# A first stage with four adaLN weight pieces loaded at once, one piece per three token tiles, and two key units among the tiles

## The reference

```
mod = silu(cond) @ ada_w + ada_b            # cond: two vectors (latent, context); ada_w: 1024 x 3072, one per layer
shift, scale, gate = split(mod, 3)
h = rmsnorm(x, norm_w) * (1 + scale) + shift
p = h @ w_in                                # the projection: per key/value head k, v, then queries and gates
```

## Time and profile before

| | |
|---|---|
| median of 3 runs | 2668.88 us |
| lowest, highest | 2666.84, 2669.97 us |
| profiled execution | 2663.45 us, of which the span of the profile 2661.6 us |
| TensorE products busy | 2588.9 us, 97% |
| TensorE weight loads busy | 2268.2 us, 85% |
| VectorE | 1187.3 us, 45% |
| ScalarE | 894.4 us, 34% |
| GpSimd | 646.4 us, 24% |
| first 1/40 of the span (66.5 us) | TensorE 6 tenths, clock 8 tenths, DMA engines 9 tenths |

### The profile page before, as it was taken

How to read it: one execution, slowest core, us unless ns; L and a number is a source line. 1 busy time by engine, 2 the same in 40 slices (tenths; PEclk the granted TensorE clock), 3 DMA queues, 4 the chain that set the end, 5 groups by cost and what they waited for, 6 DMA issues and landing times. The chain is left out here.

```text
span 2661.6 us, 49945 instructions
## 1 busy us (share of the span) xinstructions
PE 2588.9 (97%) x18699; PEld 2268.2 (85%) x18699; DVE 1187.3 (45%) x3262; ACT 894.4 (34%) x2110; POOL 646.4 (24%) x833
## 2 busy tenths in 40 slices
PE   6899999999999999999999999999999999999998
PEld 3688888888889887787999999999999999998786
DVE  3646646465464656552233342514233342515433
ACT  3445626345362654222222131312222131313211
POOL 2522131232213212332022130403122030403332
PEclk8999999999999999999999999999999999999999
DMA  9512031120212214442022220313122120416443
GB/s 358 212 51 78 17 90 30 53 79 29 74 36 71 61 56 151 135 135 74 23 50 80 38 83 18 85 44 74 47 48 82 38 83 17 86 43 163 159 144 110
DMA packets 187838, 219.66 MB, mean 83 GB/s; under 512 B 27248, under 2 KB 132480, under 8 KB 185680
## 3 DMA queue, kind: packets, MB, share of 16 engines
q1 hardware_dynamic: 177616, 189.11, 25.4%
q10 hardware_dynamic: 9984, 27.37, 2.7%
HBM read 178.27 MB, written 38.17 MB: 81 GB/s over the span
## 5 line engine op out<-in xcount | busy, mean ns | idle before, releaser
L521 PE MATMUL psum<-h_hi,m_w_lo 128*128 128x384 f32 (+1 forms) x1600 | 594.0, 371 | 1.1 <-ACT gt_nat L1408 1.1
L523 PE MATMUL psum<-h_hi,m_w_hi 128*128 128x384 f32 (+1 forms) x1600 | 573.7, 359 | 0.0
L522 PE MATMUL psum<-h_lo,m_w_hi 128*128 128x384 f32 (+1 forms) x1600 | 573.1, 358 | 0.0
L523 PEld LDWEIGHTS psum<-h_hi,m_w_hi 128*128 128x128 f32 x1600 | 300.5, 188 | 27.0
L521 PEld LDWEIGHTS psum<-h_hi,m_w_lo 128*128 128x128 f32 x1600 | 301.3, 188 | 26.0 <-issue 1.6
L522 PEld LDWEIGHTS psum<-h_lo,m_w_hi 128*128 128x128 f32 x1600 | 301.6, 189 | 22.5
L521 PE MATMUL psum<-h_hi,attn_w_lo 128*128 128x384 f32 (+1 forms) x800 | 291.9, 365 | 0.9 <-DVE attn_w_lo L506 0.6
L523 PE MATMUL psum<-h_hi,attn_w_hi 128*128 128x384 f32 (+1 forms) x800 | 285.7, 357 | 0.0
L522 PE MATMUL psum<-h_lo,attn_w_hi 128*128 128x384 f32 (+1 forms) x800 | 285.5, 357 | 0.0
L894 ACT ACTIVATE arena<-arena,stats 128x640 f32<-128x640 f32 (+2 forms) x272 | 213.4, 786 | 74.0 <-DVE stats L976 73.0
L976 DVE CUSTOM_DVE_ANT_0 arena<-psum,wmask,stats 128x640 f32<-128x640 f32 (+2 forms) x256 | 206.1, 839 | 58.7 <-PE psum L1172 58.2
(11 more groups left out here) (317 smaller groups left out, 4669.1 us busy)
## 6 DMA issues: line engine op xcount, KB each, us to landing
m_bc<-gate_rows_mlstm SPq DMA_DIRECT2D x128, 256.0 KB, 3.4
m_w_raw<-in_mlstm_w_in SPq DMA_DIRECT2D x40, 512.0 KB, 4.7
h_full<-gated_output SPq DMA_DIRECT2D x29, 512.0 KB, 4.1
gated_output<-gT SPq DMA_DIRECT2D x8, 1088.0 KB, 5.2
layer_output<-xb_out ACTq DMA_DIRECT2D x17, 512.0 KB, 2.7
h_hi_full<-layer_output SPq DMA_DIRECT2D x17, 512.0 KB, 4.8
out<-h_hi_full ACTq DMA_DIRECT2D x17, 512.0 KB, 4.9
xb<-in_x_sample ACTq DMA_DIRECT2D x16, 512.0 KB, 6.7
```

What stands on the lines that cost most here:

```text
L521: pe.matmul(out, self.lo[:, k, :], E.h_hi[:, k, tok], start=(k == 0), stop=False)
L522: pe.matmul(out, self.hi[:, k, :], E.h_lo[:, k, tok], start=False, stop=False)
L523: ins = pe.matmul(out, self.hi[:, k, :], E.h_hi[:, k, tok], start=False, stop=(k == KT - 1))
```

## The change

What it does, in order of the code:

- Pieces 0 to 3 have four buffers: the two old ones and two parts of `h_lo` that no tile has filled yet (`unborn`); SP issues all four without a wait. Pieces 4 to 7 use the old pair in turn, 8 the first of it, 9, 10 and 11 all the second (`used_by` says whose product each load waits for).
- SP's order: pieces 0 to 3, first projection weights, biases, sinks, 4, 5, turned keys, 6, 7, mask, 8, gate row, query weights, 9, then (after piece 8's product) the tables of key groups 0 and 1, biases, 10, tables 2 to 4, 11.
- TensorE: piece 1 directly behind piece 0; transposes of tiles 0 and 1 and turn 2 ahead of piece 3. Then one piece behind every third tile (4 behind tile 5, 5 behind 8, 6 behind 11, 7 behind 14), its turn one tile later. Key unit 0 stands behind tile 7, key unit 1 behind tile 12.
- Behind tile 16: piece 8, key unit 2, turn 8, piece 9, key unit 3, turn 9, key unit 4, piece 10, query unit 0, turn 10, query unit 1, piece 11, query unit 2, turn 11, values turned, query unit 3, keys turned, query unit 4. The banks of these units are chosen so that they don't meet (`unit_bank` for kv 0).
- VectorE: within a tile low_part(n-1) now stands ahead of reciprocal(n+3). The copies of pieces 9, 10 and 11, `mods(1)` and the last gate rows stand between the rotations of key and query groups; the keys' low parts come behind query groups 3 and 4.
- ScalarE: tiles 4 and 5 are loaded ahead of the modulation; for the first head the keys' high parts come after all five groups.
- GpSimd rounds the first projection weights at tile 2 instead of tile 12.

The diff, cut to its core:

```diff
-    ada = [E.arena[:, 3:7, :].rearrange("p a (b m) -> p (a b) m", m=512), take("ada1", [P, KT, 512])]
+    pair = [E.arena[:, 3:7, :].rearrange("p a (b m) -> p (a b) m", m=512), late("ada1", [P, KT, 512])[:, :, :]]
+    unborn = [E.h_full[:, :, x * P:(x + 4) * P] for x in (8, 12)]
+    ada = pair + unborn + [pair[j] for j in (0, 1, 0, 1, 0, 1, 1, 1)]
+    used_by = (None, None, None, None, 0, 1, 4, 5, 6, 7, 9, 10)
...
+    CHUNK_BEHIND = {5: 4, 8: 5, 11: 6, 14: 7}
+    def load_chunk(sp, n):
...
+        if used_by[n] is not None:
+            sp.wait_ge(s_prod, used_by[n] + 1)
+        sp.dma_start(ada[n], ...).then_inc(s_ada[n % 4], 16)
...
+    def sync(sp, load_sinks):
+        for n in range(4):
+            load_chunk(sp, n)
+        for c0, src in attn_kv_columns(E, 0):
+            sp.dma_start(raw[:, :, c0:c0 + HD], src).then_inc(s_raw, 16)
+        load_bias(sp, 0)
+        load_sinks()
+        load_chunk(sp, 4)
+        load_chunk(sp, 5)
+        sp.wait_ge(s_ckc, 1)
+        sp.dma_start(E.ckt_dram, ckt).then_inc(s_cko, 16)
+        load_chunk(sp, 6)
+        load_chunk(sp, 7)
...
+        load_chunk(sp, 8)
+        sp.wait_ge(s_grow, 2)
+        sp.dma_start(E.gates_dram[0], grow[0]).then_inc(s_gst, 16)
...
+        for n in range(NT):
             modulate(n)
+            if n >= 1:
+                low_part(n - 1)
+            if n + AHEAD < NT:
                 reciprocal(n + AHEAD)
-            if n >= 1:
-                low_part(n - 1)
...
+            if n + 1 in CHUNK_BEHIND:
+                copy_rows(CHUNK_BEHIND[n + 1])
+            if n in (6, 9):
+                gate_row(CHUNK_BEHIND[n - 1])
         low_part(NT - 1)
+        copy_rows(8)
...
         transposes(0)
         transposes(1)
+        turn(2)
+        chunk(3)
         turn(3)
-        for n in range(4, 12):
-            chunk(n)
-            if n > 4:
-                turn(n - 1)
-            for t in tiles_with(n):
-                transposes(t)
+        for t in range(2, NT):
+            transposes(t)
+            if t in CHUNK_BEHIND:
+                chunk(CHUNK_BEHIND[t])
+            if t - 1 in CHUNK_BEHIND:
+                turn(CHUNK_BEHIND[t - 1])
+            if t == 7:
+                first_keys(0)
+            if t == 12:
+                pe.wait_ge(s_row, 4)
+                first_keys(1)
...
+                load_weights(0, 1)
+                S.load_chunk(sp, 9)
+                S.sync_ropes(sp)
                 rotary(0, 0, 0)
                 rotary(0, 0, 1)
+                S.load_bias(sp, 1)
+                S.load_chunk(sp, 10)
...
                     for g in range(2, NG):
                         rotary(kv, 0, g)
+                    if kv == 0:
+                        S.load_chunk(sp, 11)
...
+                                if kv == 0 and g == 2:
+                                    copy_rows(9)
+                                if kv == 0 and g == 3:
+                                    mods(1)
+                                if kv == 0 and g == 4:
+                                    copy_rows(10)
...
+                S.chunk_of(pe, 8)
+                pe.wait_ge(S.s_ha, NS)
+                pe.wait_ge(S.s_hd, NS)
+                first_keys(2)
+                S.turn_of(pe, 8)
+                S.chunk_of(pe, 9)
+                first_keys(3)
+                S.turn_of(pe, 9)
...
+                first_keys(4)
+                S.chunk_of(pe, 10)
+                unit(0, 1, 0)
+                S.turn_of(pe, 10)
+                unit(0, 1, 1)
+                S.chunk_of(pe, 11)
+                unit(0, 1, 2)
+                S.turn_of(pe, 11)
+                values_turned(0)
+                unit(0, 1, 3)
+                keys_turned(0)
+                unit(0, 1, 4)
```

More of the change, by code:

```diff
@@ L111, in settle, with first_stage @@
     eng.sem_inc(E.s_tick, 1)
-def first_stage(E, take, s_first_lo):
+def first_stage(E, s_first_lo):
     nc = E.nc
+    tiles_only, gate_take, columns, late = (Shelf(nc, E.attn_where + x) for x in (0, 18432, 22528, 32000))
     sem = lambda n: E.semaphore(n)
@@ new lines, in first_stage, with load_bias @@
+    CHUNK_BEHIND = {5: 4, 8: 5, 11: 6, 14: 7}
+    def load_chunk(sp, n):
+        layer, c = n // 6, n % 6
+        w = E.a["attn_ada_w"] if layer == 0 else E.a["mlstm_ada_w"]
+        if used_by[n] is not None:
+            sp.wait_ge(s_prod, used_by[n] + 1)
+        sp.dma_start(ada[n], w[0].rearrange("(p k) m -> p k m", k=KT)[:, :, c * 512:(c + 1) * 512]).then_inc(s_ada[n % 4], 16)
+    def load_bias(sp, layer):
+        b = E.a["attn_ada_b"] if layer == 0 else E.a["mlstm_ada_b"]
+        for r in range(2):
+            sp.dma_start(gbias[layer][r:r + 1, :], b[:, 2 * D:3 * D]).then_inc(s_bias, 16)
@@ L240, in stats @@
             act.activation(std[:, n:n + 1], ss[:, n:n + 1], ACT.Sqrt, bias=E.eps[:, 0:1], scale=1.0 / D).then_inc(s_std, 1)
-        for n in range(NX):
-            if n == 3:
-                act.wait_ge(s_ckt, 2)
+        for n in range(3):
             load(n)
         act.wait_ge(s_silu, 2)
-        for n in range(AHEAD):
-            stats(n)
+        stats(0)
+        act.wait_ge(s_ckt, 2)
+        load(3)
+        stats(1)
+        stats(2)
+        for n in range(2):
+            act.wait_ge(s_tp, n + 1)
+            load(n + NX)
         act.wait_ge(s_mod, 1)
-        act.wait_ge(s_cko, 16)
         for n in range(NT):
             act.wait_ge(s_tp, n + 1)
-            if n + NX < NT:
+            if 2 <= n and n + NX < NT:
                 load(n + NX)
@@ L373, in turn_of @@
         if is_gate(n):
-            pe.matmul(rowps[n % 2][0:2, :], sel[:, :], rows[n % 2][:, :], start=True, stop=True).then_inc(s_gsum, 1)
+            pe.matmul(row_bank(n)[0:2, :], sel[:, :], rows[n % 2][:, :], start=True, stop=True).then_inc(s_gsum, 1)
             return
@@ L426, in tensor @@
         turn(1)
-        chunk(3)
-        turn(2)
         pe.wait_ge(s_ckc, 1)
@@ L848, in _ @@
                             ins.then_inc(s_kdup, 1)
-                        if kv == 0 and g == 0:
-                            act.wait_ge(S.s_gst, 32)
+                        if kv == 0:
+                            continue
                         act.wait_ge(s_kdup, at(kv * NG + g + 1))
                         act.copy(k_hi[:, keys_part(g)], kT[:, keys_part(g)]).then_inc(s_khi, 1)
+                    if kv == 0:
+                        act.wait_ge(S.s_grow, 4)
+                        act.wait_ge(S.s_gst, 16)
+                        act.wait_ge(s_kdup, at(NG))
+                        for g in range(NG):
+                            act.copy(k_hi[:, keys_part(g)], kT[:, keys_part(g)]).then_inc(s_khi, 1)
                     act.wait_ge(s_pv, at(kv * (2 * NT)))
@@ L1273, in _ @@
                             unit(kv, 0, g)
-                    for g in range(NG):
+                    for g in range(NG if kv else 0):
                         unit(kv, 1, g)
```

205 lines of the change are left out of this document (95 added, 110 removed).

## The result

The changed kernel takes 2671.50 us (median of 18 runs, 2667.99 to 2675.25), the kernel before beside it 2667.15 (18 runs): ratio 1.0016, 95% interval 1.0010 to 1.0023. It is 4.4 us slower. The forecast was 0.3 us faster; its range (2659 to 2677) held the time, its "no change" did not: the difference is small, but it is there.

What follows compares the result with a forecast made beforehand. TensorE, 97% busy, bounds the kernel, leaving its idle time and slow clock to win. 17.25 us to win less 16.9 lost (13.7 idle, 3.2 clock) is 0.3 us faster: 2668.6 us, range 2659 to 2677.

Steps and rivals of the forecast that it cites:

- The start: Up to the end of turn 3: four pieces at once end it at about 40.7 us, gain 1.4 us.
- still half under the transposes: Upper bound of the start: with the clock still half under the transposes, turn 3 ends at 43.5 us.
- Rival C: Start: four pieces at once gain nothing, turn 3 ends at 42 or later, 1.4 to 2.8 us slower; 0.47 with forecast.
- The filling: First tiles, 40.7 to 61.0 us: ScalarE's 2.95 us per tile sets the pace, TensorE idles 5.3 us.
- The shared port: VectorE and GpSimd exclude each other in the tile loop; at 0.3 us a tile, 2 us in the filling.
- rival B: Tile loop: token tiles come too late, 4.1 us a tile, 11.4 us lost, 2680 us; chance 0.22.
- Tiles 8 to 16: Tile loop with two key units: TensorE has most work, idle 0 (bound 3), tile 16 ends at 98.9 us.
- Turn 9: Behind the tiles: piece 9's row copy waits for key group 2's table behind piece 10; TensorE idles 7.0 us.
- tables that aren't held: In rival A (chance 0.31): without tables held behind the piece, the wait at turn 9 is 4.1 us.
- The clock at turn 9: Behind the wait at turn 9 TensorE's clock falls to half, costing 3.2 us; 0 if it doesn't fall.
- Later waits: Pieces 10 and 11 among query units: 0.5 before piece 11, 0.5 to 0.7 before query unit 3, sum 1.2 us.
- The swap: Tile loop: low part ahead of the reciprocal opens the 4.22 us ring per tile; ScalarE's 2.95 is next limit.

Runs made afterwards that it cites:

- experiment 3: Changed kernel with adaLN pieces 2 and 3 requested only when pieces 0 and 1 are used; ratio 1.0026 to the kernel before.
- Experiments 6: Changed kernel with ten throwaway identity products on TensorE behind turn 3; ratio 1.0017 to the kernel before.
- 9: Changed kernel, group 2's table ahead of piece 10, piece 9's rows copied behind key group 1, GpSimd's key-weight cast ahead of its loop; 0.9979 of kernel before.
- experiment 10: As 9, with ten throwaway identity products on TensorE behind turn 3 besides; ratio 0.9976 to the kernel before.
- experiment 2: Changed kernel with 24 throwaway identity products on TensorE between key unit 3 and turn 9; ratio 1.0016 to the kernel before.
- experiment 5: Changed kernel with the copy of piece 9's rows behind the rotation of key group 1, not group 2; ratio 1.0000 to the kernel before.
- experiment 1: Changed kernel with key group 2's table requested ahead of piece 10, not behind it; ratio 1.0007 to the kernel before.

## Why the prediction was wrong, step by step

It forecast no change, and the kernel is 4.4 us slower, clear of the noise. Its sum puts the turning of the keys at 154.65; the changed kernel's profile has 160.84, 6.2 later, and the gate unit another 1.1 later. By its steps:

- **The start (end of turn 3 at 40.7): too early.** The cached keys came at 24 as said. The end was 42.8 in this profile (2.1 late), 41.8 in the mean of ten; the gain on the old start is 0.8, not 1.4. What decides is when the clock comes back: in three profiles near 31 us, with turn 3 at 39.2 to 39.3, in others near 37, with turn 3 at 42.3 and 42.5. The bound "still half under the transposes" was drawn, and I took the other side. Rival C is half right: experiment 3 shows no gain of four pieces at once.
- **The filling (20.3 us, 5.3 of them idle): this is the step that failed.** It took 22.9 (2.6 more), 22.7 in the second profile. I had counted VectorE's low half of the key weights and left out GpSimd's high half, which the same edit moves from the thirteenth tile to the third, ahead of the diagonal that TensorE needs next; and with piece 4 moved away nothing covers the wait for the first modulation, 2.56 us, so that the clock falls, once always and, behind the wait for the diagonal, a second time in three of eight profiles. I looked for that fall only at turn 9. Experiments 6, 9 and 10 show both terms; without them the filling is the 20.3 of the sum. Of the 2.6, 0.9 are the cast; most of the rest is the second fall, which both profiles of the changed kernel had, and five of the six others with the same cast and diagonal had not.
- **The shared port.** In the text it stood at 0.3 us a tile on the side of rival B and not in the sum. The diagonal took 1.70 and 1.57 us where it met a subtraction of VectorE (the low part of a tile, that of the key weights) and 0.60 alone, and GpSimd's cast took 1.87 beside the low part and 1.04 alone. The Trainium skill, page "SBUF — State Buffer" (shared port pair), says that a GpSimd instruction that reads SBUF and a VectorE instruction with two SBUF inputs exclude each other; these rows agree. At the tile where the filling stalls the diagonal was 1.1 us longer by it. No run prices that apart from the cast: in experiment 10, with the cast gone, the same diagonal came at 52.94, ahead of the low part, and took 0.60.
- **Tiles 8 to 16 (37.9 us, idle 0): right in length.** 38.1 us, of which TensorE was idle 1.2, not 0 (1.03 for a row copy at 87), with as much less work than counted; 37.4 to 38.4 in seven others; 39.7 and 40.3 in experiments 2 and 5, where the clock fell once at 85. Rival B's ring of two periods didn't come.
- **Turn 9: right in mechanism, 1.1 late.** T to turn 9 took 21.4, not 20.3; the wait was 7.55, not 7.0, with the named releaser. The wait's end is set by the table: piece 10 was requested at T+9.6 (113.34), not T+9.1, and the multiply that waits for the table behind it starts at T+19.5, not T+18.5. Key unit 3 ends at T+13.9, 0.6 late, and so the wait is only 0.5 longer than forecast. The 4.1 that the text gives for tables that aren't held is the 3.53 of experiment 1. What the prediction did not see is the second way of experiment 5.
- **The clock at turn 9 (3.2): right**, 3.1. Turn 9 to the keys took 35.65; the sum leaves 35.45.
- **Later waits (1.2): right in sum by luck.** Ahead of piece 11 it was 0.28 (0.5 forecast), ahead of query unit 3 nothing (0.5 to 0.7). But the high and low parts of the keys, which the text put at 0 because the scores need them only 15 us later, cost 0.97 ahead of the first gate unit. The reason given looked at who needs them, not at what stands behind them on VectorE.
- **The swap: right in mechanism** (the text gives it no price of its own). 5 us in the changed kernel, 2.6 in the kernel before, where the transfers take over. Moving pieces behind the tiles is what lets the swap pay more, and it costs the waits that the moved pieces bring.

Start 2.1, filling 2.6, tiles 0.2, turn 9 1.1, rest 0.2: 6.2; with the 1.1 ahead of the gate unit 7.3. By the medians the miss is 4.7 (4.4 slower, not 0.3 faster): the start is 1 us better in the mean of ten profiles, and the second fall in the filling doesn't come in each.

The sum's terms of gain (17.3) and loss (16.9) nearly cancelled: an error of 2% of either turns the sign, and the miss of 4.7 is about a quarter. The misses of the single steps all go the same way. What came lies at 0.16%, inside the 0.2% that I had set as the bound of what can be told; with 18 runs of each kernel it can be told.

## What to carry to other kernels

A step that is moved takes the parts of all engines along: count the cast on GpSimd as well as the subtraction on VectorE, and ask which tile's small operation stands behind each. When a piece of TensorE work is moved out of a gap, the gap comes back as idle time and perhaps as a slow clock; put something there (worth 0.8 us in experiment 10 against 9, nothing in 6, where another wait took over). Work whose result nobody needs soon is free only if nothing urgent stands behind it on its engine. And a late load reaches the bound engine by every queue that stands behind its user: taking away the first wait shows only the next (experiment 5), so follow the load, not the wait.

## What the runs showed of the hardware that I had not expected

**The clock falls after short waits too, and not by their length alone.** In every profile with the wait of 2.56 us ahead of tile 2 the granted clock fell to 0.50; in the eight whose clock record shows the moment it did so 0.3 to 1.5 us into the wait (in the changed kernel turn 3 ends at 42.83 and the clock is 0.61 in the stretch 43 to 44), so that its length can't be all that counts. Behind that of 1.8 to 2.2 us ahead of tile 5 it fell in three of eight. In experiment 2 a wait of 1.00 us at 83 was followed, 1.4 us of work later, by 3 us at half clock:

```profile
84.00:86.00 2.00, 2.00 (x10) 1.64 (x10) 1.96 (x6) 1.68 (x5) 1.49 (x1) 0.88 1.05 402
86.00:88.00 2.00, 2.00 (x6) 1.60 (x5) 2.00 (x5) 1.03 (x3) 1.74 (x3) 0.50 1.05 406
```

The kernel before, run again, waited 2.77 us ahead of a tile at 58.6 and kept its clock (the second fence is the stretch behind it):

```profile
58.61 2.02 PE L407 MATMUL psum<-diag,xb 128*128 128x128 f32 x16 [2.77 <-ACT htmp L259]
```

```profile
58.00:66.00 8.00, 5.53 (x41) 3.37 (x42) 6.25 (x11) 4.52 (x12) 4.49 (x4) 1.00 1.08 365
```

In the same profile the clock fell behind a shorter wait, 2.09 us at 94:

```profile
94.29 3.29 PE L407 MATMUL psum<-diag,xb 128*128 128x128 f32 x16 [2.09 <-ACT htmp L259]
```

**Part of the scatter of whole runs arises at the start.** Turn 3 starts anywhere from 39.2 to 42.5 us with the same instructions ahead of it, by when the clock comes back. That is three quarters of the effect of this change, and the reason why the stretch behind it, which repeats within 0.5 us, told more than the times. It is not all: the two profiles of the changed kernel turn the keys at 160.84 and 160.83, and their spans are 2673.4 and 2667.1 us.
